# Modulation vectors of a two-block transformer: the product on VectorE, the sum over blocks on GpSimd

## The chip, the core and the metric

One core of one Trainium2 chip. The metric is the device time of one execution in microseconds (us), the median of three runs. Engines are called as the profile calls them: PE (TensorE's matmuls) and PEld (its weight loads), DVE (VectorE), ACT (ScalarE), POOL (GpSimd), SP (SyncE, which issues the DMAs). A matmul here has 128x128 weights and up to 512 columns.

## What is computed

A transformer block with sparse and latent attention, and behind it a second block whose norms and residuals are modulated by vectors that depend on a conditioning vector `c` (for the tokens) and `c_ctx` (for the context). The part that the change touches:

```
mod_lat = silu(c)     @ w_mod + b_mod        # w_mod: 1024 x 9216
mod_ctx = silu(c_ctx) @ w_mod + b_mod
ml, mc  = split(mod_lat, 9), split(mod_ctx, 9)
x  = x  + 0.5 * ml[2] * swiglu(modulate(rms_norm(x,  g), ml[0], ml[1]), w_in, w_out)
cx = cx + 0.5 * mc[2] * swiglu(modulate(rms_norm(cx, g), mc[0], mc[1]), w_in, w_out)
```

These two vector-matrix products depend on nothing that the first block computes, so the kernel does them while the first block runs: a feed-forward layer (ffn1), attention with its projections, `w_out`, and a second feed-forward layer (ffn2). All arithmetic is float32; the large matmuls are done as three passes on a high part and a low part of each operand.

## The kernel before

**Weights.** A weight tile of 128x2048 comes from memory into `RAW` (SP). ACT copies it rounded into `WH` (line 1080), DVE writes the rest `RAW - WH` into `WL` (line 1361, in `split`). Then PE runs on it. There are two buffers of each; while PE runs step b, ACT and DVE make the weights of step b + 1.

**Steps.** ffn1 and ffn2 have 34 steps each. `gate_up` is a step that makes one block of 128 hidden units (48 matmuls of 512 columns); after it ACT applies silu (line 1126, into `SA`), DVE multiplies (line 1437, into `VA`, which frees the PSUM banks), and POOL splits the result into `HH` (line 1845) and `HL` (line 1847). `down` (`pairs` on PE and SP) is a step that adds two blocks of the output to `X` (DVE, line 1460). The order is: 8 gate_up, 4 down, 8 gate_up, 4 down, 6 gate_up, 4 down; the last four have 36 matmuls, all others 48. Between ffn1 and ffn2 stand the attention and the four down steps of `w_out`.

**Norms.** During the last four down steps of a layer ACT squares the finished blocks of `X` (line 1095) and POOL adds six of these squares to the first (`norm`, line 1871). PE sums over partitions when the last addition is there (line 610); the next layer waits for that.

**Modulation vectors.** `w_mod` is cut into 72 tiles of 1024x128, held in `MW` as 128 partitions x 8 blocks x 128 columns. Each of the 34 steps of ffn1, the 4 of `w_out` and the 34 of ffn2 takes one tile. The first 46 tiles are multiplied by both vectors (`CV2[:, k, 0]` and `CV2[:, k, 1]`), the last 26 by one. The function `mods` exists on four engines:

- SP loads tile m + 2 into `MW` when tile m is done (semaphore `mod_s`);
- DVE, at the head of its step, multiplies block k by the scalar of each partition and adds it to the sum in `MACC` (a view of `RB`): one instruction of 128x128 for each block and vector, line 1417 for the first block and 1414 for the other seven. Each k waits for the one before;
- PE, behind the matmuls of its step, sums `MACC` over partitions (line 690, `pe.wait_ge(mod_s, ...)` at line 687), and then begins the next step;
- DVE copies the result into `MOD` at the end of its step (`mods_out`, line 1425), behind the semaphore `mod_done` of PE.

**Order.** Every engine runs its instructions in the order in which they are written, and `stage` makes rolled loops of most of them. So on DVE a step is: `mods`, `split`, the work on PE's result, `mods_out`. POOL has only `hidden` in a gate_up step, and nothing in a down step but the additions of `norm`, which stand behind a layer's last `hidden`.

Of the kernel before, what the change touches and what calls it, by code (L numbers as in the profile page):

```python
# [4 lines left out]
P = 128  # L5
# [54 lines left out]
def build(nc, inp, out):  # L60
    ctx = ExitStack()
    with ctx:
# [100 lines left out]
        mod_loaded = [sem(f"mod_loaded{s}") for s in range(2)]  # L163
        mod_s = sem("mod_s")
        mod_done, mod_out = sem("mod_done"), sem("mod_out")
# [68 lines left out]
        NCTX = 5 * KD  # L234
        MACC = RB[:, :].rearrange("p (t v c) -> p t v c", t=2, v=2)

        def vectors(m0):

            return 2 if m0 < NCTX else 1
# [209 lines left out]
        def _(sp):  # L449
# [8 lines left out]
            def mods(b0, j, s, m0):  # L458

                if m0 is None:  # L460
                    return
                if b0 == 0 and isinstance(j, int) and j < 2:
                    if j == 1:
                        for t in range(2):
                            sp.dma_start(MW[t][:, :, :], weights(inp["w_mod_2"][0], 0, KD, t * P, P))\
                                .then_inc(mod_loaded[t], 16)
                    return
                t = (s + b0) % 2
                if m0 == M0["wo"]:
                    sp.wait_ge(at_o, NG)  # L470
                if not (isinstance(j, int) and j + m0 < 2):
                    sp.wait_ge(mod_s, j * KD + KD * (m0 - 1))
                sp.dma_start(MW[t][:, :, :], weights(inp["w_mod_2"][0], 0, KD, j * P + m0 * P, P))\
                    .then_inc(mod_loaded[t], 16)
# [33 lines left out]
            for n in range(10):  # L508
                b = w_in_b + n
                s = b % 2  # L510
                sp.wait_ge(w_lo, b - 1)
                raw = RAW[s][:, :].rearrange("p (h k c) -> p h k c", h=2, k=KD)
                for half, (name, j, c) in enumerate(W_IN_TILES[2 * n:2 * n + 2]):
                    for c0, width, at in (MISC if name == "misc" else ((c, P, 0),)):
                        sp.dma_start(raw[:, half, :, at:at + width],
                                     w_in[:, c0:c0 + width].rearrange("(k p) n -> p k n", p=P)).then_inc(w_loaded[s], 16)
                if n == 0:
                    sp.wait_ge(pe_done, w_in_b)
                    sp.wait_ge(mod_s, KD * M0["wo"])
                    for dst, src in ((TA, "rope64"), (TB, "rope96"), (PERM, "perms")):  # L520
                        sp.dma_start(dst[:, :, :], inp[src]).then_inc(a_loaded, 16)
                    sp.dma_start(CM[:, :], inp["causal"]).then_inc(a_loaded, 16)
# [44 lines left out]
        def _(pe):  # L567
# [114 lines left out]
            def mods(b0, j, s, m0):  # L682
# [3 lines left out]
                t = (s + b0) % 2  # L686
                pe.wait_ge(mod_s, j * KD + KD * (m0 + 1))
                wait(pe, mod_out, after(j + m0, -1))
# [666 lines left out]
        def _(dve):  # L1355
# [46 lines left out]
            def mods(b0, j, s, m0):  # L1402
# [4 lines left out]
                dve.wait_ge(mod_loaded[t], j * 8 + (8 * (m0 - t) + 16))  # L1407
                for k in range(KD):
                    if k:
                        dve.wait_ge(mod_s, j * KD + (KD * m0 + k))  # L1410
                    for v in range(vectors(m0)):
                        o = MACC[:, t, v, :]
                        if k:
                            last = dve.scalar_tensor_tensor(out=o, in0=MW[t][:, k, :], scalar=CV2[:, k, v:v + 1],  # L1414
                                                            in1=o, op0=ALU.mult, op1=ALU.add)
                        else:
                            last = dve.tensor_scalar(o, MW[t][:, k, :], CV2[:, k, v:v + 1], None, ALU.mult)
                    last.then_inc(mod_s, 1)

# [418 lines left out]
        def _(pool):  # L1838
            def hidden(b0, n, tok, g0):

                for b, j, s, _ in stage(pool, b0, n):
                    pool.wait_ge(psum_free, b + 1)
                    h = HH[:, ds(j, 1), 0:tok].rearrange("p a t -> p (a t)")
# [4 lines left out]

            def ffn(stages, tok, g0):
                for kn, (bg, bd) in zip(CHUNKS, stages):  # L1850
                    hidden(bg, kn, tok, g0)
                    g0 += kn

            def branch(b0, h_to, l_to, y0):
# [9 lines left out]

            def norm(m):

                for k in range(1, m.n - 1):
                    pool.wait_ge(norm_sq, m.sq + k + 1)
# [15 lines left out]
            lows(norm1)  # L1884
            ffn(ffn1, T, 0)
            norm(norm_mix)
            lows(norm_mix)
            pool.wait_ge(ix_acc, 3 * IDX_HEADS)
            pool.memset(VB[:, :, :, :], 0.0).then_inc(v_zero, 1)
            norm(norm2)  # L1890
            lows(norm2)
            ffn(ffn2, T, H0["ffn2"])
            norm(norm_final)
            ffn(ffn3, T + TC, H0["ffn3"])
            norm(norm_x2)
            branch(bg_b, YH, YL, 0)
            branch(ba_b, MH, ML, KD)
            norm(norm_x3)
            ffn(ffn4, T, H0["ffn4"])
            norm(norm_out)  # L1900

# [72 lines left out]
```

## Time and profile before

| | |
|---|---|
| median of 3 runs | 2821.77 us (2820.44 to 2825.56) |
| the profiled execution | 2822.73 us, of which the span in the trace is 2820.9 us |
| PE busy | 2709.4 us (96%) |
| DVE, ACT, POOL busy | 1421.5, 757.6, 346.7 us |

The span is the time from the first to the last instruction in the trace; the 1.8 us around it are in the measured time too. "Busy" adds the durations of an engine's instructions. A timeline row gives the start in us from the span's start, the duration in us (of all instructions that it merges), engine, line, operation, what it writes and reads, and in brackets how long the engine had stood idle before and what ended that. An instruction's duration includes what it waits inside for memory ports.

### The profile page before, as it was taken

The page shows a single profiled execution, that of the slowest core. Times are in us where ns is not written, and L with a number is a line of the kernel's source. Part 1 is how long each engine was busy: PE and PEld are TensorE (multiplying, and loading weights), DVE is VectorE, ACT ScalarE, POOL GpSimd, SP SyncE. Part 2 cuts the span into 40 slices and gives each one's busy share as a digit, 9 for nine tenths or more (in the row PEclk, how much of TensorE's full clock was granted, in tenths as well). Part 3 has the DMA queues.
Part 4 walks back from the last instruction along what each step waited for, and adds up shares of the span by engine and source line. Part 5 has one row for each costly group of instructions (what it writes and reads, how often), then busy time and mean ns, then how long its engine had stood idle before and what let it go on. Part 6 is the DMA issues. An engine that isn't in the chain of part 4 may idle for free.

```text
span 2820.9 us, 34194 instructions
## 1 busy us (share of the span) xinstructions
PE 2709.4 (96%) x12500; PEld 2168.7 (77%) x12500; DVE 1421.5 (50%) x2491; ACT 757.6 (27%) x1029; POOL 346.7 (12%) x259
## 2 busy tenths in 40 slices
PE   8999989888899999998999999999999999999998
PEld 6888877644457888878888888878888756888887
DVE  7877784556647756673122222254324653433333
ACT  3111232235542112133111111222322352321213
POOL 2111120000002101111211301200200002210102
PEclk9999999869699999987999999999999999999999
DMA  6444432200034454431212221222332001323331
GB/s 181 135 134 144 135 116 74 54 15 1 0 102 115 135 142 147 130 109 37 67 60 60 60 75 56 64 75 90 90 105 83 31 1 60 90 90 98 96 97 67
DMA packets 394763, 241.12 MB, mean 85 GB/s; under 512 B 14768, under 2 KB 392752, under 8 KB 394672
## 3 DMA queue, kind: packets, MB, share of 16 engines
q1 hardware_dynamic: 394672, 239.92, 29.1%
q8 instruction: 55, 0.90, 0.1%
q14 instruction: 36, 0.29, 0.0%
HBM read 237.79 MB, written 2.10 MB: 85 GB/s over the span
## 4 chain that ended last, share of the span: by engine, by line
PE 88%; DVE 7%; ACT 4%; issue 1%; DMA 1%; POOL 0%; SPq 0%; DVEq 0%; ACTq 0%; POOLq 0%
PE PS L669 22%; PE PS L676 21%; PE PS L671 21%; PE PS L656 3%; PE PS L653 3%; PE PS L654 3%; PE PS L1053 2%; PE PS L810 1%; PE PS L610 1%; DVE RB L1414 1%; PE PS L1033 1%; PE PS L896 1%; DVE WL L1361 1%; PE PS L876 1%; PE PS L903 1%
## 5 line engine op out<-in xcount | busy, mean ns | idle before, releaser
L669 PE MATMUL PS<-NH,WH 128*128 128x512 f32 (+1 forms) x2128 | 626.0, 376 | 10.6 <-DVE WL L1361 6.3
L671 PE MATMUL PS<-NH,WL 128*128 128x512 f32 (+1 forms) x2128 | 620.1, 373 | 0.0
L676 PE MATMUL PS<-NL,WH 128*128 128x512 f32 (+1 forms) x2128 | 591.5, 372 | 0.0
L1361 DVE TENSOR_TENSOR WL<-RAW,WH 128x2048 fp32r<-128x2048 f32 x190 | 462.0, 2432 | 103.6 <-ACT WH L1080 103.1
L1080 ACT ACTIVATE WH<-RAW 128x2048 fp32r<-128x2048 f32 x190 | 363.7, 1914 | 540.0 <-PE PS L676 501.0
L669 PEld LDWEIGHTS PS<-NH,WH 128*128 128x128 f32 x2128 | 384.0, 189 | 79.3 <-issue 9.0
L671 PEld LDWEIGHTS PS<-NH,WL 128*128 128x128 f32 x2128 | 389.3, 189 | 72.2
L676 PEld LDWEIGHTS PS<-NL,WH 128*128 128x128 f32 x2128 | 389.5, 189 | 71.9
L1414 DVE SCALAR_TENSOR_TENSOR RB<-MW,CV,RB 128x128 f32<-128x128 f32 x826 | 329.2, 431 | 17.8
L1126 ACT ACTIVATE SA<-PS 128x512 f32<-128x512 f32 x104 | 62.0, 596 | 663.1 <-PE PS L676 630.6
L669 PE MATMUL PS<-HH,WH 128*128 128x512 f32 (+1 forms) x820 | 237.5, 371 | 1.9 <-DVE WL L1361 1.9
L671 PE MATMUL PS<-HH,WL 128*128 128x512 f32 (+1 forms) x820 | 235.1, 368 | 0.0
L1845 POOL CAST HH<-VA 128x512 f32 (+2 forms) x88 | 58.6, 666 | 1332.3 <-DVE VA L1437 1332.3
L676 PE MATMUL PS<-HL,WH 128*128 128x512 f32 (+1 forms) x820 | 222.1, 368 | 0.0
L1437 DVE TENSOR_TENSOR VA<-SA,PS 128x512 f32<-128x512 f32 x88 | 60.4, 686 | 245.5 <-ACT SA L1126 245.5
L1847 POOL TENSOR_TENSOR HL<-VA,HH 128x512 f32 (+2 forms) x88 | 168.5, 1914 | 14.2 <-POOL HH L1845 14.0
L676 PEld LDWEIGHTS PS<-HL,WH 128*128 128x128 f32 x820 | 148.8, 189 | 26.6
L671 PEld LDWEIGHTS PS<-HH,WL 128*128 128x128 f32 x820 | 148.5, 188 | 26.6
L669 PEld LDWEIGHTS PS<-HH,WH 128*128 128x128 f32 x820 | 146.1, 188 | 25.9 <-DVE WL L1361 2.1
L1436 DVE TENSOR_TENSOR VA<-SA,PS 128x256 f32<-128x256 f32 x22 | 9.3, 421 | 271.7 <-ACT SA L1126 271.7
L653 PE MATMUL PS<-NH,WH 128*128 128x512 f32 x320 | 127.3, 398 | 0.0
L654 PE MATMUL PS<-NL,WH 128*128 128x512 f32 x320 | 122.2, 384 | 0.0
(268 smaller groups left out, 2691.6 us busy)
## 6 DMA issues: line engine op xcount, KB each, us to landing
RAW<-in_ffn_w_in SPq DMA_DIRECT2D x88, 512.0 KB, 4.8
MW<-in_w_mod SPq DMA_DIRECT2D x72, 512.0 KB, 3.7
RAW<-in_w_in SPq DMA_DIRECT2D x70, 512.0 KB, 4.1
RAW<-in_w_gate SPq DMA_DIRECT2D x44, 512.0 KB, 4.2
RAW<-in_w_up SPq DMA_DIRECT2D x44, 512.0 KB, 5.4
RAW<-in_w_down SPq DMA_DIRECT2D x32, 512.0 KB, 4.3
RAW<-in_ffn_w_out SPq DMA_DIRECT2D x32, 512.0 KB, 4.3
RAW<-in_w_out SPq DMA_DIRECT2D x16, 512.0 KB, 4.4
```

The costliest lines, as they stand in the source:

```text
L653: pe.matmul(o, wh, xh(k), start=k == 0, stop=False)
L654: pe.matmul(o, wh, xl(k), start=False, stop=False)
L656: last = pe.matmul(o, wl, xh(k), start=False, stop=k == kn - 1)
L669: pe.matmul(outs[half][x], w[half][0], xh(k), start=k == 0, stop=False)
L671: pe.matmul(outs[half][x], w[half][1], xh(k), start=False, stop=False)
L676: last = pe.matmul(outs[half][x], w[half][0], xl(k), start=False, stop=k == kn - 1)
L1080: act.activation(WH[1 - s][:, :], RAW[1 - s][:, :], ACT.Copy).then_inc(w_hi, 1)
L1126: act.activation(SA[:, s, 0:T], G[s][:, :], func).then_inc(gate_done, 1)
L1361: dve.tensor_tensor(WL[1 - s][:, :], RAW[1 - s][:, :], WH[1 - s][:, :].bitcast(F32), ALU.subtract).then_inc(w_lo, 1)
L1414: last = dve.scalar_tensor_tensor(out=o, in0=MW[t][:, k, :], scalar=CV2[:, k, v:v + 1], in1=o, op0=ALU.mult, op1=ALU.add)
L1437: dve.tensor_tensor(VA[:, s, 0:T], SA[:, s, 0:T], U[s][:, :], ALU.mult).then_inc(psum_free, 1)
L1847: pool.tensor_tensor(l, VA[:, s, 0:tok], h.bitcast(F32), ALU.subtract).then_inc(h_split, 1)
```

## The change

On DVE `mods` becomes one multiplication of 128x1024 for each vector: the whole tile times `CV2` broadcast along the 128 columns. The product with the last (or only) vector is written in place into `MW`, that with the first of two into a part of `CX`, a buffer that is otherwise not in use until ffn2 is over (`product`). It signals `mod_p`.

POOL gets a `mods` of its own: it adds the eight blocks in three halvings (4 blocks onto 4, 2 onto 2, 1 and 1 into `MACC`), for both vectors in turn, waits between the halvings for its own results (`mod_t`), and signals `mod_s` at the end. It also waits for `mod_done` of the tile before last. `mods` stands ahead of `hidden` in a gate_up step, and is all that POOL does in a down step (`down`); in the last four down steps the additions of `norm` are now written between the tiles' sums: one behind the second tile, two behind the third, three behind the fourth. The counts in the waits on `mod_s` go down from eight for each tile to one. PE's instructions stay as they are.

```diff
 # semaphores, and the place of the product
+        mod_p, mod_t, mod_s = sem("mod_p"), sem("mod_t"), sem("mod_s")
+        def product(t, v, m0):
+            return MW[t][:, :, :] if v == vectors(m0) - 1 else CX[:, 4 * t:4 * t + 4, :].rearrange("p a (b c) -> p (a b) c", b=2)
...
 # SP, mods
-                    sp.wait_ge(mod_s, j * KD + KD * (m0 - 1))
+                    sp.wait_ge(mod_s, j + (m0 - 1))
...
 # PE, mods
-                pe.wait_ge(mod_s, j * KD + KD * (m0 + 1))
+                pe.wait_ge(mod_s, j + (m0 + 1))
...
 # DVE, mods
-                for k in range(KD):
-                    if k:
-                        dve.wait_ge(mod_s, j * KD + (KD * m0 + k))
-                    for v in range(vectors(m0)):
-                        o = MACC[:, t, v, :]
-                        if k:
-                            last = dve.scalar_tensor_tensor(out=o, in0=MW[t][:, k, :], scalar=CV2[:, k, v:v + 1],
-                                                            in1=o, op0=ALU.mult, op1=ALU.add)
-                        else:
-                            last = dve.tensor_scalar(o, MW[t][:, k, :], CV2[:, k, v:v + 1], None, ALU.mult)
-                    last.then_inc(mod_s, 1)
+                for v in range(vectors(m0)):
+                    last = dve.tensor_tensor(product(t, v, m0), MW[t][:, :, :],
+                                             CV2[:, :, v:v + 1].to_broadcast([P, KD, P]), ALU.mult)
+                last.then_inc(mod_p, 1)
...
 # POOL
+            def mods(b0, j, s, m0, t0):
+
+                if m0 is None:
+                    return
+                t, nv = (s + b0) % 2, vectors(m0)
+                pool.wait_ge(mod_p, j + (m0 + 1))
+                if not (isinstance(j, int) and j + m0 < 2):
+                    pool.wait_ge(mod_done, j + (m0 - 1))
+                for n, w in enumerate((4, 2)):
+                    for v in range(nv):
+                        p = product(t, v, m0)
+                        pool.tensor_tensor(p[:, 0:w, :], p[:, 0:w, :], p[:, w:2 * w, :], ALU.add).then_inc(mod_t, 1)
+                    pool.wait_ge(mod_t, j * (2 * nv) + (t0 + (n + 1) * nv))
+                for v in range(nv):
+                    p = product(t, v, m0)
+                    last = pool.tensor_tensor(MACC[:, t, v, :], p[:, 0, :], p[:, 1, :], ALU.add)
+                last.then_inc(mod_s, 1)
...
+            def down(b0, m0, t0, m=None):
+
+                for b, j, s, _ in stage(pool, b0, KD // 2, True):
+                    mods(b0, j, s, m0, t0)
+                    if m is not None and j:
+                        norm(m, 2 * j - 2, 2 * j)
...
                 for b, j, s, _ in stage(pool, b0, n):
+                    mods(b0, j, s, m0, t0)
                     pool.wait_ge(psum_free, b + 1)
```

In the rows below the line numbers of before and after differ by a few. DVE, around the second step of ffn1, before (`RB` is where `MACC` lies, `CV` is `CV2`):

```order
L1437 TENSOR_TENSOR VA<-SA,PS 128x512
L1425 COPY MOD<-PS 128x2
L1417 TENSOR_SCALAR RB<-MW,CV 128x128 x2
L1414 SCALAR_TENSOR_TENSOR RB<-MW,CV,RB 128x128 x14
L1361 TENSOR_TENSOR WL<-RAW,WH 128x2048
L1437 TENSOR_TENSOR VA<-SA,PS 128x512
L1425 COPY MOD<-PS 128x2
```

and now:

```order
L1434 TENSOR_TENSOR VA<-SA,PS 128x512
L1422 COPY MOD<-PS 128x2
L1413 TENSOR_TENSOR CX<-MW,CV 128x1024
L1413 TENSOR_TENSOR MW<-MW,CV 128x1024
L1365 TENSOR_TENSOR WL<-RAW,WH 128x2048
L1434 TENSOR_TENSOR VA<-SA,PS 128x512
L1422 COPY MOD<-PS 128x2
```

The sixteen small instructions between the copy into `MOD` and the making of `WL` have become two large ones, and nothing else on DVE has moved.

POOL, one gate_up step in the rolled loop of ffn1, with the semaphores that the instructions wait for, before:

```order
L1845 ISA [waits psum_free]
L1845 COPY HH<-VA 128x512
L1847 REGISTER_ALU [waits pool_s]
L1847 TENSOR_TENSOR HL<-VA,HH 128x512
L1842 REGISTER_ALU
```

and now:

```order
L1847 TENSOR_TENSOR CX<-CX 128x512 [waits mod_done]
L1847 TENSOR_TENSOR MW<-MW 128x512
L1848 ISA
L1847 TENSOR_TENSOR CX<-CX 128x256 [waits mod_t]
L1847 TENSOR_TENSOR MW<-MW 128x256
L1848 REGISTER_ALU
L1851 TENSOR_TENSOR RB<-CX 128x128 [waits mod_t]
L1851 TENSOR_TENSOR RB<-MW 128x128
L1872 ISA [waits psum_free]
L1872 COPY HH<-VA 128x512
L1874 REGISTER_ALU [waits pool_s]
L1874 TENSOR_TENSOR HL<-VA,HH 128x512
```

Six additions with three waits for other work or for POOL's own results stand ahead of the split of the hidden block.

POOL, the end of ffn1, before:

```order
L1847 TENSOR_TENSOR HL<-VA,HH 128x512
L256 REGISTER_ALU
L256 COMPARE_AND_BRANCH
L1871 TENSOR_TENSOR VA<-VA,SA 128x512 [waits norm_sq]
L1871 TENSOR_TENSOR VA<-VA,SA 128x512 [waits norm_acc,norm_sq] x5
L1878 TENSOR_TENSOR NL<-VA,NH 128x512 [waits norm_hi] x3
```

and now:

```order
L1906 TENSOR_TENSOR VA<-VA,SA 128x512 [waits norm_acc,norm_sq] x2
L1847 TENSOR_TENSOR CX<-CX 128x512 [waits mod_done,mod_p]
L1847 TENSOR_TENSOR MW<-MW 128x512
L1847 TENSOR_TENSOR CX<-CX 128x256 [waits mod_t]
L1847 TENSOR_TENSOR MW<-MW 128x256
L1851 TENSOR_TENSOR RB<-CX 128x128 [waits mod_t]
L1851 TENSOR_TENSOR RB<-MW 128x128
L1906 TENSOR_TENSOR VA<-VA,SA 128x512 [waits norm_acc,norm_sq] x3
L1913 TENSOR_TENSOR NL<-VA,NH 128x512 [waits norm_hi] x3
```

The additions of squares, which stood alone behind the last split, now stand behind the sums of tiles; the last three wait behind those of the last tile.

## Rows read from the trace of the kernel before

**Rows 1.** Page, part 1: busy time, share, instructions of each engine.

```profile
PE 2709.4 (96%) x12500; PEld 2168.7 (77%) x12500; DVE 1421.5 (50%) x2491; ACT 757.6 (27%) x1029; POOL 346.7 (12%) x259
```

**Rows 2.** Timeline, TensorE, one step of ffn1: start us, us, work [idle before].

```profile
66.55 0.50 PE L690 MATMUL PS<-ones,RB 128*128 128x1 f32 x4
...
77.90 0.50 PE L690 MATMUL PS<-ones,RB 128*128 128x1 f32 x4
```

**Rows 3.** Timeline, VectorE, the same step.

```profile
67.38 0.69 DVE L1437 TENSOR_TENSOR VA<-SA,PS 128x512 f32<-128x512 f32 x1 [1.82 <-ACT SA L1126]
68.05 0.89 DVE L1417 TENSOR_SCALAR RB<-MW,CV 128x128 f32<-128x128 f32 x2
68.97 5.55 DVE L1414 SCALAR_TENSOR_TENSOR RB<-MW,CV,RB 128x128 f32<-128x128 f32 x14
74.44 2.28 DVE L1361 TENSOR_TENSOR WL<-RAW,WH 128x2048 fp32r<-128x2048 f32 x1
```

**Rows 4.** Timeline, GpSimd, the same step.

```profile
68.24 0.61 POOL L1845 CAST HH<-VA 128x512 f32 x1 [8.94 <-DVE VA L1437]
69.02 1.45 POOL L1847 TENSOR_TENSOR HL<-VA,HH 128x512 f32 x1 [0.17 <-POOL HH L1845]
```

**Rows 5.** Group of line 1414: shortest, median, longest in ns.

```profile
L1414 DVE SCALAR_TENSOR_TENSOR RB<-MW,CV,RB x826: 337/351/1493, 26.1 to 1245.7; 128x128 f32<-128x128 f32 x166
```

**Rows 6.** Timeline, VectorE and GpSimd, ffn3 and then ffn4.

```profile
1334.12 2.45 DVE L1361 TENSOR_TENSOR WL<-RAW,WH 128x2048 fp32r<-128x2048 f32 x1 [0.70 <-ACT WH L1080]
...
1334.60 3.69 POOL L1847 TENSOR_TENSOR HL<-VA,HH 128x768 f32 x1 [0.17 <-POOL HH L1845]
...
2482.89 3.35 DVE L1361 TENSOR_TENSOR WL<-RAW,WH 128x2048 fp32r<-128x2048 f32 x1 [1.03 <-ACT WH L1080]
...
2482.80 1.29 POOL L1847 TENSOR_TENSOR HL<-VA,HH 128x512 f32 x1 [0.16 <-POOL HH L1845]
```

**Rows 7.** Timeline, one 128x1024 instruction of VectorE, one of GpSimd.

```profile
13.00 1.22 DVE L1501 TENSOR_TENSOR WL<-RAW,WH 128x1024 fp32r<-128x1024 f32 x1
...
14.38 2.36 POOL L1882 TENSOR_TENSOR WL<-RAW,WH 128x1024 fp32r<-128x1024 f32 x1 [13.93 <-ACT WH L1171]
```

**Rows 8.** Timeline, start of ffn1: VectorE, then TensorE.

```profile
25.56 0.48 DVE L1417 TENSOR_SCALAR RB<-MW,CV 128x128 f32<-128x128 f32 x2 [1.65 <-ACT CV L1176]
30.51 2.28 DVE L1361 TENSOR_TENSOR WL<-RAW,WH 128x2048 fp32r<-128x2048 f32 x1
...
31.09 0.50 PE L690 MATMUL PS<-ones,RB 128*128 128x1 f32 x4
32.85 0.72 PE L669 MATMUL PS<-NH,WH 128*128 128x512 f32 x2 [1.25 <-DVE WL L1361]
```

**Rows 9.** Timeline, TensorE, last down stage of ffn1 and what follows.

```profile
372.15 0.73 PE L669 MATMUL PS<-HH,WH 128*128 128x512 f32 x2 [1.28 <-DVE WL L1361]
...
392.12 0.50 PE L653 MATMUL PS<-HH,WH 128*128 128x512 f32 x1 [1.59 <-DVE WL L1361]
...
400.45 0.61 PE L690 MATMUL PS<-ones,RB 128*128 128x1 f32 x4
405.26 1.02 PE L610 MATMUL PS<-ones,VA 128*128 128x1 f32 x4 [4.20 <-POOL VA L1871]
```

**Rows 10.** Timeline, GpSimd, squares added in that stage.

```profile
394.01 2.73 POOL L1871 TENSOR_TENSOR VA<-VA,SA 128x512 f32<-128x512 f32 x2 [7.81 <-ACT SA L1095]
```

**Rows 11.** Timeline, TensorE, w_out: first step, and after the last.

```profile
830.16 0.73 PE L669 MATMUL PS<-NH,WH 128*128 128x512 f32 x2 [0.94 <-DVE WL L1361]
...
865.98 0.72 PE L610 MATMUL PS<-ones,VA 128*128 128x1 f32 x5 [1.57 <-POOL VA L1871]
```

**Rows 12.** Timeline, TensorE, start of ffn2.

```profile
885.75 0.84 PE L690 MATMUL PS<-ones,RB 128*128 128x1 f32 x4 [2.11 <-DVE RB L1414]
888.06 1.19 PE L669 MATMUL PS<-NH,WH 128*128 128x512 f32 x2 [1.47 <-DVE WL L1361]
```

**Rows 13.** Stretches: PE, PEld, DVE, ACT, POOL busy us, PEclk, DMA share, GB/s.

```profile
888.00:892.00 4.00, 3.94 (x9) 3.13 (x10) 3.89 (x10) 0.00 (x0) 2.05 (x2) 0.50 0.91 266
```

More of the change, by code:

```diff
@@ L163, in build @@
         mod_loaded = [sem(f"mod_loaded{s}") for s in range(2)]
-        mod_s = sem("mod_s")
+        mod_p, mod_t, mod_s = sem("mod_p"), sem("mod_t"), sem("mod_s")
         mod_done, mod_out = sem("mod_done"), sem("mod_out")
@@ L518, in _ @@
                     sp.wait_ge(pe_done, w_in_b)
-                    sp.wait_ge(mod_s, KD * M0["wo"])
+                    sp.wait_ge(mod_s, M0["wo"])
                     for dst, src in ((TA, "rope64"), (TB, "rope96"), (PERM, "perms")):
@@ L1838, in _, with adds, hidden @@
         def _(pool):
-            def hidden(b0, n, tok, g0):
+            def mods(b0, j, s, m0, t0):
[14 more added lines that the diff above has]
+                last.then_inc(mod_s, 1)
+            def adds(m0, n):
+                return 0 if m0 is None else 2 * vectors(m0) * n
+            def down(b0, m0, t0, m=None):
[3 more added lines that the diff above has]
+                        norm(m, 2 * j - 2, 2 * j)
+            def hidden(b0, n, tok, g0, m0=None, t0=0):
                 for b, j, s, _ in stage(pool, b0, n):
+                    mods(b0, j, s, m0, t0)
                     pool.wait_ge(psum_free, b + 1)
@@ L1847, in hidden, with ffn @@
                     pool.tensor_tensor(l, VA[:, s, 0:tok], h.bitcast(F32), ALU.subtract).then_inc(h_split, 1)
-            def ffn(stages, tok, g0):
-                for kn, (bg, bd) in zip(CHUNKS, stages):
-                    hidden(bg, kn, tok, g0)
+            def ffn(stages, tok, g0, m=None, m0=None, t0=0):
+                for c, (kn, (bg, bd)) in enumerate(zip(CHUNKS, stages)):
+                    hidden(bg, kn, tok, g0, m0, t0)
+                    t0 += adds(m0, kn)
+                    m0 = None if m0 is None else m0 + kn
+                    if m0 is not None or c == 2:
+                        down(bd, m0, t0, m if c == 2 else None)
+                    t0 += adds(m0, KD // 2)
+                    m0 = None if m0 is None else m0 + KD // 2
                     g0 += kn
+                norm(m, KD - 2, KD - 1)
+                return t0
             def branch(b0, h_to, l_to, y0):
@@ L1863, in branch, with norm @@
                             .then_inc(y_split, 1)
-            def norm(m):
-                for k in range(1, m.n - 1):
+            def norm(m, k0=1, k1=KD - 1):
+                for k in range(max(k0, 1), k1):
                     pool.wait_ge(norm_sq, m.sq + k + 1)
@@ L1884, in _ @@
             lows(norm1)
-            ffn(ffn1, T, 0)
-            norm(norm_mix)
+            t0 = ffn(ffn1, T, 0, norm_mix, M0["ffn1"])
             lows(norm_mix)
@@ L1889, in _ @@
             pool.memset(VB[:, :, :, :], 0.0).then_inc(v_zero, 1)
-            norm(norm2)
+            down(wo_b, M0["wo"], t0, norm2)
+            t0 += adds(M0["wo"], KD // 2)
+            norm(norm2, KD - 2, KD - 1)
             lows(norm2)
[L1892 to L1895, printed above, removed]
+            ffn(ffn2, T, H0["ffn2"], norm_final, M0["ffn2"], t0)
+            ffn(ffn3, T + TC, H0["ffn3"], norm_x2)
             branch(bg_b, YH, YL, 0)
@@ L1898, in _ @@
             norm(norm_x3)
-            ffn(ffn4, T, H0["ffn4"])
-            norm(norm_out)
+            ffn(ffn4, T, H0["ffn4"], norm_out)
 def _vectors(inputs):
```

## The prediction

> **What bounds the kernel now.** I read part 1 of the page first: PE is busy for 2709 of 2821 us, DVE for half, POOL for 12% [rows 1]. Then the timeline of one ordinary step, engine by engine, then the places where PE waits.
>
> In an ordinary step PE sets the pace. It comes to the modulation matmuls at 66.55 and again at 77.90, 11.35 us later [rows 2], and waits for nothing. DVE's work on modulation in this step begins at 68.05 and is 6.4 us long; `WL` follows at 74.44 and ends at 76.72 [rows 3]. `mod_s` is thus there at 74.5, 3.4 us before PE asks, and `WL` 1.2 us before. DVE is nearly full, but not late. What leaves it earns nothing here; what comes to lie between 66.5 and 77.9 in a chain may cost.
>
> DVE is late at a few places. At the start PE is ready after 31.6 and waits 1.25 for `WL` [rows 8]. In the last down stage of ffn1, whose steps have 36 matmuls instead of 48, it waits 1.28 and 1.59, and once between them about half as long [rows 9]. In `w_out` it is 0.94 [rows 11], at the start of ffn2 2.11 and 1.47 [rows 12]. With some 2 of the 4.20 at the end of ffn1 [rows 9], where DVE makes `WL` before it finishes `X`, all that an unloaded DVE could give is about 12 us.
>
> **What DVE and POOL cost each other.** Two pairs of rows show that an instruction of DVE with two SBUF inputs and one of POOL don't overlap [rows 6]. In ffn3 `HL` was issued at 1334.60 while `WL` ran to 1336.57; it took 3.69, to 1338.29, 1.72 from the end of `WL`. In ffn4 `HL` was first, and ended at 2484.09; `WL`, issued at 2482.89, took 3.35 instead of 2.28 and ended at 2486.24, 2.15 after it. Each holds the other for its whole length; who asked first goes first. `HL` in an ordinary step waits only for one small instruction (1.45 instead of 1.29) [rows 4, 6], since DVE's are 0.35 short; but the longest of those is 1.49, an addition of POOL longer [rows 5]. I take it that an instruction which reads PSUM and one SBUF operand has no part in this. The Trainium skill says the same as a rule ("SBUF — State Buffer", section "Who interferes with whom"): the pair of ports is locked for the whole instruction when DVE has two SBUF inputs and GpSimd reads SBUF. By that rule, the trace agrees, the product of the change is such an instruction, since `CV2` lies in SBUF too.
>
> **The prices.** DVE: a 128x1024 instruction with two SBUF inputs is 1.22 [rows 7], 1.14 apart when they follow one another: 2.3 for a tile with two vectors, where 6.4 (5.0 undisturbed, 25.56 to 30.6 [rows 8]) goes away. A broadcast operand is not in the trace; it could only make this longer. POOL: 128x512 took 1.29 [rows 6], 128x1024 2.36 [rows 7], so 0.2 + 2.1 ns for each column. I have no row of 256 or 128 columns; by this line they are 0.74 and 0.47. The sum of a tile for two vectors is then 2 x (1.29 + 0.74 + 0.47) = 5.0, with two waits of POOL for itself of 0.17 [rows 4] 5.3; I use 5.1, for one vector 2.8. Bounds: the second of two additions may begin inside the first, or all be 0.1 shorter; or each small one may have a floor nearer to 512's.
>
> **Ordinary gate_up steps with two vectors.** The chain from PE's last matmul E: DVE is free for the product at E + 1.5 (68.05 against 66.55). Products with POOL's cast of 0.6 between them: to E + 4.4. `HL`, which waited at the port: to E + 5.6. `WL`, issued behind the product: to E + 7.7. Only then the sums, to E + 12.8; PE has its next matmuls done at E + 11.35. So PE waits about 1.4, and the modulation matmul moves from before anything that waits to the end of the chain. In the step behind such a late one, DVE starts the product when its copy into `MOD` is done, 0.7 behind the modulation matmul M, and the chain gives M + 11.55 against M + 11.38: 0.2 more. Two steps cost 1.6, one 0.8. There are 22 such steps in ffn1 (the first apart) and 8 in ffn2: 21 x 0.8 = 17, 7 x 0.8 = 5.5.
>
> **Down steps** have no split of POOL: products, `WL`, sums give E + 1.5 + 2.3 + 2.2 + 5.1 = E + 11.1. They just fit: 0. **Steps with one vector** have 3.4 us less: 0.
>
> **The starts.** ffn1: products 25.56 to 27.9, `WL` to 30.1, sums to 35.2, then 0.5 of modulation matmuls: PE goes on at 35.8 instead of 32.85, +3.0 [rows 8]. That DVE makes `WL` 2.5 us sooner doesn't help, because PE's modulation matmuls stand ahead of step 2. `w_out`: the same, against 830.16: +2.0. ffn2, where DVE comes to the tile behind a norm, against 888.06: +3.0.
>
> **The last down stages.** ffn1, from modulation matmul to modulation matmul. POOL now adds squares behind each sum, and these (two of 1.37, [rows 10]) take port time from the next product: 0.7 + 2 squares and 2 products in turn to 4.6, `WL` to 6.8, sums to 11.9. With one pair, with one addition and with none that is 11.9, 10.9, 10.5, in all 33.3 where the trace has 30.1 (from 372.15 - 1.28 - 0.5 to 400.45 [rows 9]); into the stage another +3.4 (12.0, where 36 matmuls and their modulation matmuls need 8.6). Behind the last one come three squares, 4.1, where the trace waits 4.8 to 405.26 [rows 9]: -0.7. Together +6.0. `w_out`: +0.9 in the last step, and 4.1 instead of 2.1 from its last modulation matmul to 865.98 [rows 11], +1.9: +2.8. ffn2, one vector: +1.9.
>
> **SP** now loads tile m + 2, and behind it the weights of the next step, when POOL has done tile m, so near the end of a step instead of its middle. They are wanted almost a whole step later, so I count 0.
>
> **Sum.** 3.0 + 17 + 6.0 (ffn1) + 2.0 + 2.8 (`w_out`) + 3.0 + 5.5 + 1.9 (ffn2) = 41. Overlap of two additions by 0.1 takes 7 off, by the same chain; all additions 0.1 shorter would take 16. On the other side PE's restart: modulation matmuls behind a wait took 0.84, otherwise 0.50 [rows 2, 12], about 0.3 in a dozen steps, +4; and the clock was at half (0.50, 1.2 GHz) at 888 to 892 after PE had stood [rows 13], so the waits at the starts, now of 4 and 6 us, may cost as much again. I take **+38**. The profiled execution (2822.73, span 2820.9) lies 1 us above the median; the forecast goes on the median: 2821.8 + 38 = **2860**.
>
> **Rivals.**
> *It costs much more.* If an addition of 256 or 128 columns costs as much as 512 on POOL, 1.3, every sum is 2.7 longer, also the down steps are late (1.9 each) and the gate_up steps 3.0: the same chain gives +145. With 0.2 more for each, +65. Against: 2.36 for 1024 leaves a fixed part of only 0.2. 12% for over +55.
> *Faster.* If the small additions slip in between DVE's instructions and PE finds `mod_s` in time, what is left is DVE's lateness, up to 12 us of it; with the last stage and the starts half won, -8, 2814. It decides at the start: the sums must be done by 32.8, 4.9 us behind the product, with `WL` in the same time and ports. The Trainium skill speaks for this side ("VectorE: DVE Perf Modes", section "Rules for kernel authors"): chained DVE instructions should become few, and the sixteen do become two. For: DVE's time falls by 200 us. Against: [rows 6] leave 5.1 + 2.2 in a row. 8%.
> *It nearly fits.* With additions 0.3 shorter than I have them, the chain of a gate_up step ends inside PE's matmuls, and only starts and ends of layers cost: +3, and up to +5.6 it can't be told from nothing. 11%.
> *Forecast*, +6 to +55: 69%.
>
> **Numbers.** Within 0.2% (5.6 us, about what a measurement of this kernel can tell from no change): 0.11. Faster by more: 0.08. Slower by more: 0.81. The range is 2824 to 2890: it leaves out the faster case, a part of the near fit, and the upper half of the costly one.
>
> **What the profile would show.** PE's wait list gets an entry for line 690 behind POOL's last addition, some 20 to 30 us in all, with waits of 1 to 1.5 in every second gate_up step with two vectors and none where one vector is left. DVE busy falls by about 200 us, POOL's rises by 250 to 300. `WL` or the additions are stretched where they meet. The start of step 2 is at 35.8. POOL's additions read 1.3, 0.74 and 0.47. I am wrong if two-vector steps of 11.35 remain (the chain is shorter than I have it), if down steps are late too (small additions have a floor), or if PE waits for weights from memory.

## The result, and the profile of the changed kernel

The changed kernel takes **2867.8 us** (2859.1 to 2870.9, 4 runs), the kernel before beside it 2821.1 (2818.9 to 2825.6). The ratio is 1.0159, 95% interval 1.0132 to 1.0185: 1.3 to 1.9% slower. The execution profiled after the change took 2870.9 us with a span of 2868.8, so 47.9 us more than the span of before.

Page, part 1, of after (answers [rows 1]):

```profile
PE 2733.5 (95%) x12500; PEld 2180.8 (76%) x12500; DVE 1244.3 (43%) x1665; ACT 757.4 (26%) x1029; POOL 821.7 (29%) x613
```

DVE has 177 us less and POOL 475 more. Of POOL's, about 290 are additions as they last undisturbed (an estimate: 46 tiles at 2 x (1.28 + 0.74 + 0.46), 26 at half of that); most of the rest is time in which an instruction of POOL stood at the memory port behind one of DVE. The groups of the new instructions, on POOL and DVE, shortest, median and longest in ns:

```profile
L1847 POOL TENSOR_TENSOR CX<-CX x92: 722/1014/3341, 28.6 to 1012.4; 128x512 f32<-128x512 f32 x46, 128x256 f32<-128x256 f32 x46
L1851 POOL TENSOR_TENSOR RB<-CX x46: 452/460/464, 34.7 to 1013.9; 128x128 f32<-128x128 f32 x46
L1413 DVE TENSOR_TENSOR CX<-MW,CV x46: 1211/1216/2221, 26.2 to 1003.9; 128x1024 f32<-128x1024 f32 x46
```

256 columns are 0.72 to 0.74 on POOL, 128 are 0.46, and the product with its broadcast operand is 1.22, as any 128x1024 instruction [rows 7].

**One gate_up step.** Timeline of after, first PE, then DVE, then POOL, from the modulation matmuls of one step to those of the next (answers [rows 2 to 4]):

```profile
48.67 0.51 PE L694 MATMUL PS<-ones,RB 128*128 128x1 f32 x4
61.16 0.61 PE L694 MATMUL PS<-ones,RB 128*128 128x1 f32 x4 [0.98 <-POOL RB L1851]
72.92 0.61 PE L694 MATMUL PS<-ones,RB 128*128 128x1 f32 x4
...
50.18 1.22 DVE L1413 TENSOR_TENSOR CX<-MW,CV 128x1024 f32<-128x1024 f32 x1
51.31 1.64 DVE L1413 TENSOR_TENSOR MW<-MW,CV 128x1024 f32<-128x1024 f32 x1
52.87 3.38 DVE L1365 TENSOR_TENSOR WL<-RAW,WH 128x2048 fp32r<-128x2048 f32 x1
...
51.95 2.15 POOL L1874 TENSOR_TENSOR HL<-VA,HH 128x512 fp32r<-128x512 f32 x1
54.06 3.33 POOL L1847 TENSOR_TENSOR CX<-CX 128x512 f32<-128x512 f32 x1
57.36 1.29 POOL L1847 TENSOR_TENSOR MW<-MW 128x512 f32<-128x512 f32 x1
58.73 0.74 POOL L1847 TENSOR_TENSOR CX<-CX 128x256 f32<-128x256 f32 x1
...
60.65 0.46 POOL L1851 TENSOR_TENSOR RB<-MW 128x128 f32<-128x128 f32 x1
```

Read it as one row at a port. `HL` is issued while the second product runs (to 52.95) and ends 1.15 behind it, at 54.10. `WL`, issued at 52.87, ends 2.15 behind `HL`, at 56.25. The first addition, issued at 54.06, lasts 3.33, because it ends 1.14 behind `WL`. Then the other five follow, and PE, ready at 60.2, goes on at 61.16. The step has taken 12.49 us instead of 11.35; the one behind it takes 11.76 and shows no wait.

**Where the 47.9 us are.** Distances to the same instruction of before, at the modulation matmuls and the sums of the norms:

| stretch | forecast | measured |
|---|---|---|
| start of ffn1, to the second tile | 3.0 | 4.8 |
| two-vector gate_up steps of ffn1 | 17 | 16.4 |
| two-vector down steps of ffn1 | 0 | 0.0 |
| last down stage of ffn1, to the norm's sums | 6.0 | 6.7 |
| attention | 0 | -0.5 |
| `w_out`, start | 2.0 | 4.9 |
| `w_out`, rest, to the norm's sums | 2.8 | 2.2 |
| norm2 and start of ffn2 | 3.0 | 5.9 |
| two-vector steps of ffn2 | 5.5 | 5.2 |
| one-vector steps of ffn2 | 0 | 0.0 |
| last down stage of ffn2, to the norm's sums | 1.9 | 1.2 |
| all behind it | 0 | 0.9 |

The starts are larger than forecast. Timeline of PE in after, the first tile of ffn1, of `w_out`, and of ffn2 (answers [rows 8], [rows 11], [rows 12]), and of the stretches behind the three waits (busy us of PE, PEld, DVE, ACT, POOL, then PEclk; answers [rows 13]):

```profile
35.59 0.61 PE L694 MATMUL PS<-ones,RB 128*128 128x1 f32 x4 [3.74 <-POOL RB L1851]
...
858.96 1.01 PE L694 MATMUL PS<-ones,RB 128*128 128x1 f32 x4 [2.52 <-POOL RB L1851]
...
927.07 1.00 PE L694 MATMUL PS<-ones,RB 128*128 128x1 f32 x4 [6.05 <-POOL RB L1851]
```

```profile
35.50:40.00 4.50, 4.41 (x14) 3.56 (x15) 3.77 (x4) 0.00 (x0) 2.13 (x4) 0.62 0.76 217
859.00:866.00 7.00, 7.00 (x19) 5.70 (x20) 4.63 (x4) 1.67 (x3) 3.48 (x2) 0.51 0.74 218
927.00:935.00 8.00, 7.93 (x23) 6.41 (x24) 5.11 (x4) 0.00 (x0) 5.46 (x4) 0.56 0.74 197
```

In all three TensorE was granted half its clock (1.2 instead of 2.4 GHz) for most of the stretch, which makes the means of 0.51 to 0.62 above; before, the clock was full at the first two. At the start of ffn1 a part of the 4.8 is no effect of the change: the first product began at 26.17, where the first multiplication of before began at 25.56, because PE had waited 5.9 us for the input instead of 5.1.

### The profile page after: what moved, and what is told of

It is laid out like the page before. It is cut to its first block, busy times and chain, and to the rows that moved or that the text cites. A ratio compares the mean times of both kernels' runs of the same rounds, so it can differ in the third digit from the quotient of the medians.

```text
span 2868.8 us, 33435 instructions
## 1 busy us (share of the span) xinstructions
PE 2733.5 (95%) x12500; PEld 2180.8 (76%) x12500; DVE 1244.3 (43%) x1665; ACT 757.4 (26%) x1029; POOL 821.7 (29%) x613
## 4 chain that ended last, share of the span: by engine, by line
PE 75%; issue 9%; POOL 6%; DVE 6%; ACT 3%; DMA 1%; DVEq 0%; POOLq 0%; SPq 0%; ACTq 0%
PE PS L673 19%; PE PS L680 19%; PE PS L675 19%; POOL CX L1847 3%; PE PS L657 2%; PE PS L660 2%; PE PS L658 2%; POOL MW L1847 2%; PE PS L1057 2%; PE PS L614 1%; PE PS L1037 1%; DVE MW L1413 1%; PE PS L880 1%; PE PS L900 1%; DVE VA L1399 1%
## 5 line engine op out<-in xcount | busy, mean ns | idle before, releaser
L1365 DVE TENSOR_TENSOR WL<-RAW,WH 128x2048 fp32r<-128x2048 f32 x190 | 486.1, 2559 | 106.1 <-ACT WH L1084 105.6
L1872 POOL CAST HH<-VA 128x512 f32 (+2 forms) x88 | 85.9, 977 | 843.2 <-DVE VA L1434 843.2
L1847 POOL TENSOR_TENSOR CX<-CX 128x512 f32<-128x512 f32 x92 | 182.4, 1982 | 294.0 <-DVE MW L1413 290.4
L1874 POOL TENSOR_TENSOR HL<-VA,HH 128x512 f32 (+2 forms) x88 | 214.1, 2433 | 14.4 <-POOL HH L1872 14.2
L1847 POOL TENSOR_TENSOR MW<-MW 128x512 f32<-128x512 f32 (+1 forms) x144 | 171.5, 1191 | 58.6 <-DVE MW L1413 56.6
```

The source lines that it names most:

```text
L1365: dve.tensor_tensor(WL[1 - s][:, :], RAW[1 - s][:, :], WH[1 - s][:, :].bitcast(F32), ALU.subtract).then_inc(w_lo, 1)
L1847: pool.tensor_tensor(p[:, 0:w, :], p[:, 0:w, :], p[:, w:2 * w, :], ALU.add).then_inc(mod_t, 1)
L1872: pool.tensor_copy(h, VA[:, s, 0:tok]).then_inc(pool_s, 1)
L1874: pool.tensor_tensor(l, VA[:, s, 0:tok], h.bitcast(F32), ALU.subtract).then_inc(h_split, 1)
```

## The experiments

All times are medians of four to eleven runs; the kernel before ran beside each (2820.9, 2820.2 and 2820.8 in the three groups). The last column of the table is read from the profiles: how much later than in the kernel before PE ends the matmuls of ffn2's last step. What lies behind that is the same code in all. It took 1565 to 1575 us in the profiles of this case, so a difference between two spans is no finer than some us, and this column is finer.

| kernel | us | ratio to before (95%) | at ffn2's end |
|---|---|---|---|
| changed | 2867.8 | 1.0132 to 1.0185 | +46.6 |
| one_vector | 2816.6 | 0.9976 to 1.0002 | -7.1 |
| halving_out | 2820.0 | 0.9992 to 1.0020 | +2.2 |
| halving_twice | 2921.3 | 1.0339 to 1.0374 | +100.2 |
| sums_on_dve | 2820.3 | 0.9986 to 1.0005 | +0.7 |
| pe_later | 2819.9 | 0.9985 to 1.0012 | +3.0 |
| first_on_dve | 2828.5 | 1.0014 to 1.0045 | +9.1 |
| filled_waits | 2856.8 | 1.0102 to 1.0144 | +37.1 |
| first_on_dve_later | 2818.0 | 0.9973 to 0.9999 | -3.2 |
| later_wl_first | 2850.7 | 1.0094 to 1.0122 | +29.0 |
| half_later_wl_first | 2824.9 | 0.9999 to 1.0018 | +7.5 |
| dve_later_wl_first | 2823.1 | 0.9994 to 1.0018 | +0.2 |
| before_later_wl_first | 2818.9 | 0.9985 to 1.0004 | +0.9 |

**The length of the chain.** The theory (A): PE asks for a sum that ends a row of instructions at the port, and that row is 1.4 us too long. The rival (B): the loss goes with the time that POOL's work adds.

```diff
 # one_vector, for DVE and POOL
-            return 2 if m0 < NCTX else 1
+            return 1
 # halving_out
-                for n, w in enumerate((4, 2)):
+                for n, w in enumerate((4,)):
 # halving_twice
-                for n, w in enumerate((4, 2)):
+                for n, w in enumerate((4, 2, 2)):
```

> The changed kernel, but only one vector is multiplied and added for every tile; PE keeps both of its modulation matmuls and sums the same row twice (the vectors for the context are left out of what is computed). Theory A: PE waits because product, WL and sums run in a row at the memory port (E + 12.8 us against a step of 11.35, E being PE's last matmul of the step before). Here the row is 1.14 + 2.5 us shorter, E + 9.1, so the waits of all gate_up steps go (21.6 us as measured: 16.4 in ffn1, 5.2 in ffn2), most of the 4.5 at the start and of the 6.7 at the end of ffn1, and some 8 around w_out and the start of ffn2: 2826 us (2815 to 2835), PE's waits for POOL's sums under 5 us in all. Theory B: what costs is that POOL's and DVE's instructions are stretched by each other, in proportion to the time that POOL adds. Half of the additions are left: 2868 - 46/2 = 2845 us.

> The changed kernel without its second halving (256 columns); blocks 2, 3, 6 and 7 are left out of the sums. Theory A (a chain that is 1.4 us too long): two additions of 0.74 are 1.5 us, and the chain ends at E + 11.3, just inside the step. The 21.6 us of the gate_up steps go, and 1.5 us at each of about six late places (three starts, the last down steps of ffn1, w_out): 2868 - 21.6 - 9 = 2837 us (2830 to 2843). Theory B (in proportion to POOL's added time, of which 30% goes): 2868 - 14 = 2854 us.

> The changed kernel with its second halving done twice (the sums hold two of the partial sums twice, so the vectors are others). Theory A: the chain is 1.5 us longer, now late in every gate_up step with two vectors: from modulation matmul to modulation matmul 11.55 + 1.5 = 13.05 us, where the two lengths of now have a mean of 12.1. 28 steps give 27 us; 8 down steps, until now just in time, 0.45 each, 4 us; the last down stage of ffn1 4.5, w_out 3, three starts 4.5; steps with one vector nothing. 2868 + 43 = 2911 us (2900 to 2920). Theory B: + 14, 2882 us.

A holds and B falls: 1.5 us off a sum of 5 gave back 48 us, 1.5 us more cost 53. The waits of PE that end with a sum, in the kernel without the second halving and in that with two:

```profile
PE PS L694 <- POOL RB L1851: 10.9, 5, 4.6
```

```profile
PE PS L694 <- POOL RB L1851: 68.8, 35, 8.0
```

(us in total, times, longest; in the changed kernel 31.3, 25 and 6.0.) Without the halving the 28 gate_up steps cost 1.1 us instead of 21.6. With two, I had every late step at 13.05 and came out 10 too low, and the clock is the likely reason. Two steps behind a wait of 1.92 ran at full clock (1.00 from 207 to 232.9), in 12.80 and 13.25, as expected. But in much of ffn1 and in ffn2 steps of 14.0 and 13.1 alternate, with waits of 2.5 to 2.6 in every second one, and behind most of these the clock was half for some 3 to 4 us. One of them, PE, POOL's last addition for the next tile, and the stretch behind the wait:

```profile
260.29 0.61 PE L694 MATMUL PS<-ones,RB 128*128 128x1 f32 x4 [2.60 <-POOL RB L1851]
273.45 0.50 PE L694 MATMUL PS<-ones,RB 128*128 128x1 f32 x4
...
272.55 0.46 POOL L1851 TENSOR_TENSOR RB<-MW 128x128 f32<-128x128 f32 x1
...
260.30:266.00 5.70, 5.70 (x20) 4.60 (x21) 4.71 (x4) 0.00 (x0) 3.16 (x3) 0.70 0.72 218
```

The step takes 13.16 though its sum is done at 273.01, before PE has done its matmuls: PE at half clock sets it, not the chain. Such a pair is 27.1, the one at full clock 26.05; ten waits in gate_up steps (1.6 to 2.6 us) had the half clock behind them, and at about 1 us each they are the 10 us (an estimate from these two pairs; no run fills these waits). The other misses have one sign too: what the shorter chain saved outside the gate_up steps was 24 us, not 9, above all 14 between the end of ffn1 and the start of ffn2. More on this below.

**The products or the sums.**

```diff
 # sums_on_dve: behind the products, on DVE; POOL has no mods
+                dve.wait_ge(mod_p, j + (m0 + 1))
+                for n, w in enumerate((4, 2)):
+                    for v in range(nv):
+                        p = product(t, v, m0)
+                        dve.tensor_tensor(p[:, 0:w, :], p[:, 0:w, :], p[:, w:2 * w, :], ALU.add).then_inc(mod_t, 1)
...
```

> The products as in the changed kernel, but all three halvings on DVE, and POOL has no modulation work; the additions of the norms stay where the changed kernel has them on POOL. It tells the large products (and their broadcast operand, and the new place of the norms' additions) from the move of the sums to POOL. Theory A: DVE's modulation work for two vectors is 2.3 + 2 x (0.65 + 0.37 + 0.22) + 0.2 of waits = 5.0 us, about what the sixteen small ones take undisturbed and 1.4 less than they take beside HL, and ends before WL: no wait of PE for sums. 2820 us (2812 to 2828). Rival: the products themselves, longer at the port than 0.35 us each, are what delays HL, WL and PE: then it stays over 2840 us.

As expected: the large products and the broadcast operand cost nothing, nor do the norms' additions in their new place as long as no sums stand in front of them; the move of the sums does. But DVE wins no time by them either. Its timeline, one two-vector tile in this kernel:

```profile
68.55 1.22 DVE L1413 TENSOR_TENSOR CX<-MW,CV 128x1024 f32<-128x1024 f32 x1
69.69 1.63 DVE L1413 TENSOR_TENSOR MW<-MW,CV 128x1024 f32<-128x1024 f32 x1
71.36 1.66 DVE L1422 TENSOR_TENSOR CX<-CX 128x512 f32<-128x512 f32 x1
...
74.86 2.28 DVE L1365 TENSOR_TENSOR WL<-RAW,WH 128x2048 fp32r<-128x2048 f32 x1
```

6.3 us from the first product to `WL`, where the sixteen small instructions took 6.4 [rows 3]: 0.5 and 1.0 of it is waiting behind POOL's cast and `HL`, which come between long instructions as between short ones.

**The place where PE asks.**

```diff
 # pe_later: PE (and DVE's copy into MOD alike)
             def mods(b0, j, s, m0):
-                t = (s + b0) % 2
...
+                if not (isinstance(j, int) and j + m0 in STARTS):
+                    sums(b0 - 1, j, s, m0 - 1)
+                if isinstance(j, int) and j + m0 in ENDS:
+                    sums(b0, j, s, m0)
```

> The changed kernel; PE's two modulation matmuls of tile m, and DVE's copy of their result, stand one step later, behind the matmuls of step m + 1 (the last tile of ffn1, of w_out and of ffn2 stays behind its own step). All work is the same, only the place at which PE asks for the sums. Theory A (PE loses time because it asks at the end of a chain that is 1.4 us too long): the 21.6 us of the gate_up steps go, 4.5 at the start, and some 5 at the starts of w_out and ffn2; the last down stages keep their loss, since the last tile is asked for at once. 2868 - 31 = 2837 us (2828 to 2845), two-vector steps of 11.35 to 11.45. Rival: product, WL, HL and sums together fill the memory port for 11.4 us of a step of 11.35, so that the steps stay above 11.7 wherever PE asks: over 2848 us.

The 21.6 us are gone, and so is the rival. Three of PE's modulation matmuls, and one first addition on POOL:

```profile
201.16 0.50 PE L704 MATMUL PS<-ones,RB 128*128 128x1 f32 x4
212.51 0.51 PE L704 MATMUL PS<-ones,RB 128*128 128x1 f32 x4
223.87 0.50 PE L704 MATMUL PS<-ones,RB 128*128 128x1 f32 x4
...
206.64 3.33 POOL L1863 TENSOR_TENSOR CX<-CX 128x512 f32<-128x512 f32 x1
```

The same work at the same port (the first addition of most tiles still lasts 3.2 to 3.3, of the others 1.3) fits into steps of 11.35. The forecast of 2837 was too high; the start gave 6.4 instead of 4.5, and from the end of ffn1 to the start of ffn2 12 came back instead of 5.

**The clock.** Three long waits stand in front of stretches at half clock. Filled with matmuls that nobody reads:

```diff
 # filled_waits: FILL = {0: 16, NF + 12: 10, M0["ffn2"]: 24}
+                if isinstance(j, int) and j + m0 in FILL:
+                    busy(FILL[j + m0])
                 pe.wait_ge(mod_s, j + (m0 + 1))
```

> The changed kernel; where PE waits 3.7, 2.5 and 6.1 us for the first tile of ffn1, of w_out and of ffn2, it first does 16, 10 and 24 matmuls of 128 columns that nobody reads. In the changed kernel the granted clock was 0.5 (1.2 GHz) for 3.4, 7 and 6 us after these waits. If the clock falls because PE stood idle, the matmuls behind run at full clock, and half of that time comes back, less what the filling overruns: 5 to 8 us less, 2861 us. Rival (the clock falls at such places anyway, as it also did at 888 us before): no difference, 2867 to 2870 us.

11 us less, and the granted clock behind all three places was full: at these places the clock falls because PE stands, and the rival falls. The stretches of this kernel that answer to those of after:

```profile
35.50:40.00 4.50, 4.50 (x23) 3.77 (x23) 4.06 (x4) 0.00 (x0) 2.12 (x3) 1.00 0.84 230
856.50:863.00 6.50, 6.50 (x30) 5.38 (x30) 4.63 (x4) 0.72 (x2) 3.88 (x2) 1.00 0.79 238
921.00:929.00 8.00, 8.00 (x38) 6.69 (x38) 5.62 (x4) 0.00 (x0) 5.46 (x4) 1.00 0.74 197
```

From these tiles' modulation matmuls to the next ones it is 11.47, 11.47 and 11.46, where the changed kernel has 13.08, 14.68 and 14.75. By place, in the profiles, the gain is 1.9 at the start (0.3 of it ahead of the first tile), 5.5 between the end of ffn1 and the second tile of ffn2, and 2.1 in the last down stage of ffn1, where nothing was filled: behind a wait of 2.94 the changed kernel had its half clock there too (0.53 at 395 to 402), this one, behind a wait of 2.88, did not. So a wait of that length can go either way, as in halving_twice above.

**Sharing the sums.** The first halving on DVE (in the second kernel with PE's matmuls one step later, and the norm's additions ahead of the sums):

```diff
 # first_on_dve, behind the products on DVE; POOL: enumerate((2,))
+                for v in range(vectors(m0)):
+                    p = product(t, v, m0)
+                    last = dve.tensor_tensor(p[:, 0:4, :], p[:, 0:4, :], p[:, 4:8, :], ALU.add)
+                last.then_inc(mod_p, 1)
 # first_on_dve_later, also: POOL, down
+                    if m is not None and j:
+                        norm(m, 2 * j - 2, 2 * j)
                     mods(b0, j, s, m0, t0)
```

> The changed kernel with the first halving (512 columns) on DVE right behind the products, and the second and third on POOL. The row of a two-vector tile is two additions of 1.29 shorter on POOL and two of 0.65 and a wait of 0.1 longer on DVE, 1.2 us less in all. By Theory A as it stands after the kernel without the second halving (1.5 us less: 2820) it is nearly enough: a wait of 0.2 is left in some gate_up steps, 3 us, and the late places cost 2 more: 2825 us (2820 to 2832). Rival: the long additions on DVE push HL and WL back by what they take off the sums, and it stays near the changed kernel, over 2845 us.

> The first halving on DVE and PE's modulation matmuls one step later together, and in the last down stages POOL's additions for the norm ahead of the tile's sums. Theory A: PE waits for no sum but at three ends of layers; the port is filled 10.2 us of 11.35, so WL and HL are in time. What is left against the kernel of before is the gain of an earlier WL at the start, at w_out and in the last down steps (4 us, as with one vector): 2816 us (2810 to 2822), a little faster than before. Rival (the port or DVE's longer row delay WL or HL): 2825 us or more.

Both as expected by A. With the halving shared, two-vector steps alternate between 11.5 and 11.35. With PE's question a step later as well no sum is late but at the ends of layers, the steps of 36 matmuls run in 8.63 (before: 8.64, 10.06, 9.52, 10.50), and the kernel's median is 2.2 us under that of before (ratio of the runs 0.9986, interval 0.9973 to 0.9999). It is the only one whose interval lies under 1, by a hair, and one of twelve such intervals may do so by chance: a gain is not shown. What the norm's additions ahead of the sums add isn't told apart either, since no run has them alone.

**The order on DVE.** In four kernels `split` stands ahead of `mods` and PE's matmuls one step later: with all sums on POOL, with the shared halving, with all on DVE, and with the instructions of the kernel before. The first three also have the norm's additions ahead of the sums.

```diff
 # DVE, gate_up and down
-                    mods(b0, j, s, m0)
                     split(s, b)
+                    mods(b0, j, s, m0)
```

> The changed kernel with PE's modulation matmuls one step later, DVE making WL ahead of the products, and POOL's additions for the norm ahead of the tile's sums in the last down stages. With the matmuls one step later alone: 2819.9. What the order adds: no product ahead of WL where DVE is late (in front of the first step of w_out and of ffn2, 1 to 2 us each), and squares that don't wait for 5 us of sums. 2816 us (2811 to 2821). Rival: HL and the products now come behind 2.3 us of WL, the port is as full as before, and nothing is won: 2820 us.

> The same with the first halving on DVE. Without WL first it was 2818.0. The gain of WL first as above, 2 us: 2816 us (2810 to 2820). If it is POOL's load that holds the ends of ffn1 and w_out, it is 2 us under the kernel with all sums on POOL; if DVE's lateness does, 2 us over it.

> Products and all sums on DVE (2820.3 in the old order), with PE's modulation matmuls one step later and WL first. PE's waits of before, 1.25 at the start, 1.3 + 1.6 + 0.7 in the last down stage of ffn1, 0.9 in w_out, 2.1 + 1.5 at ffn2, were waits for WL behind 5 to 6.4 us of modulation work. With WL first they go: 2820 - 8 = 2812 us (2808 to 2817). Rival (the gain comes from unloading DVE): over the kernels with sums on POOL.

> The kernel of before, sixteen small instructions for a tile and all, with only the two changes of order: PE's modulation matmuls one step later, WL first on DVE. If the order is what gains, and neither the products nor POOL's sums, it is as fast as the three kernels above: 2821 - 8 = 2813 us (2808 to 2818). Rival: the changed kernel's lighter DVE is worth 3 us or more beside it.

None gains what I expected, and the first is 31 us slower than pe_later, which has the product first (and the norm's additions behind the sums; first_on_dve_later has them ahead and loses nothing). Its timeline, ACT and then DVE in one step, and SP's issue of the tile and the weights:

```profile
210.52 1.92 ACT L1094 ACTIVATE WH<-RAW 128x2048 fp32r<-128x2048 f32 x1 [7.05 <-DMA RAW<-in_w_up]
...
212.47 2.29 DVE L1375 TENSOR_TENSOR WL<-RAW,WH 128x2048 fp32r<-128x2048 f32 x1 [8.12 <-ACT WH L1094]
...
203.09 0.37 SPq L480 DMA_DIRECT2D MW<-in_w_mod  x1
203.73 0.37 SPq L488 DMA_DIRECT2D RAW<-in_w_gate  x1
204.20 1.01 SPq L490 DMA_DIRECT2D RAW<-in_w_up  x1
```

DVE waits 8 us for `WH`, ACT 7 us for weights from memory. SP loads a tile when POOL's sum is done (`mod_s`), and the weights stand behind it in its queue. With `WL` first the sum ends later, the weights are late by as much, `WL` is late, and the products behind it make the next sum late. This is read from the timeline; no run gives the tiles another queue to test it. In PE's waits it shows as 25.7 us for sums, in 7 waits, most of it at the ends of ffn1 and `w_out`. ACT's waits for weights of gate, up and down in this kernel and in pe_later (us in total, times, longest):

```profile
ACT WH L1094 <- DMA RAW<-in_w_up: 137.8, 25, 15.5
ACT WH L1094 <- DMA RAW<-in_w_down: 101.6, 16, 12.9
```

```profile
ACT WH L1094 <- DMA RAW<-in_w_up: 18.7, 9, 5.9
ACT WH L1094 <- DMA RAW<-in_w_down: 11.7, 1, 11.7
```

In the changed kernel neither is there. The two kernels with all modulation work on DVE do win PE's waits for `WL`: they end the matmuls of the last step of ffn1 5.5 and 6.1 us earlier than before. They give it back to the last tile, whose sum is wanted at once: PE waits 6.5 and 6.1 us for it. That the lighter DVE gives nothing beside the order isn't shown by them, since with one_vector, where both engines have half the work, 7 us came by the last column (4 in the medians, with an interval that still holds 1).

## Why the prediction held, and where it was off

**The chain.** It was put at products E + 4.4, `HL` + 5.6, `WL` + 7.7, sums + 12.8; the step above has 4.3, 5.4, 7.6 and 12.4 (E = 48.67). The late step was put at 11.55 behind the modulation matmul and took 11.76. The pair is 24.25 against 24.35, 0.77 us for a step where 0.8 was said; that it is so close is partly luck, since the early step was put 0.3 too long and the late one 0.2 too short. Down steps fit, one-vector steps fit, both as said. In the first stage of ffn1 the waits are spread more evenly (steps of 12.0 to 12.3 behind the first pair), at the same sum.

**The rule on the port.** [rows 6] showed one engine held for the whole instruction of the other, and the 3.38 of `WL` and 3.33 of the addition are that again. The Trainium skill ("SBUF — State Buffer", section "Who interferes with whom") states it, and the trace agrees. With both engines always asking, the order in the step shown is alternate, each taking the port when the other's instruction ends, which is why DVE's `WL` didn't have to wait for all six additions, nor they slip in front of it.

**The rule on few instructions.** The rival "faster" rested on fewer instructions on DVE. The Trainium skill asks for that ("VectorE: DVE Perf Modes", section "Rules for kernel authors"). The runs show next to no gain from it: undisturbed, two products and six additions are 2.3 + 2.5 us against 5.0 for the sixteen, since a multiplication and an addition are now two instructions over the same columns; and sums_on_dve is as fast as before. The point from which that rival decided was the start: sums by 32.8. They ended at 35.53, 35.2 forecast.

**POOL's prices.** 1.29, 0.74 and 0.47 from a line through two rows; 1.28, 0.74 and 0.46 measured. The costly rival (a floor under small additions) and the near fit both needed other prices. The sums are 4.85 long behind `WL` where 5.1 was taken. For that, an overlap by 0.1, the forecast took 7 us off; but the late steps came out 0.2 longer than forecast and gave it back. The 7 off is the one term of the sum that found nothing to stand on: the pair is that of the 41.

**The starts: the term that was too small.** At the start of ffn1 PE went on at 36.06 where 35.8 was said, but what followed, mostly at half clock, cost 1.6 more. For PE's restart and the clock 4 us were written, and the clock itself was left to words ("may cost as much again"). filled_waits prices it at about 7.4 at the three places, and 9.5 with the fourth. By the table the three starts are 7.6 over their terms, and all else together is 1.1 under. That the forecast came out at 38 and not at 41 is the 7 taken off in vain, less those 4.

**Signs named beforehand.** PE's entry for the sum behind POOL's: 20 to 30 us said, 31.3 found, with waits of 0.8 to 1.1 in every second gate_up step (1 to 1.5 said), and in the first stage and in ffn2 shorter ones in almost every step. POOL +250 to 300 was said, +475 found: the record of an instruction counts its time at the port, which the forecast of this sign forgot though it had said it of [rows 4]. DVE -200 said, -177 found, for the same reason.

**SP.** Counted at 0, with "wanted almost a whole step later" as the cover. It held in the changed kernel. pe_later and above all later_wl_first show what that cover hides: a queue in which weights stand behind a wait for the sum.

**Still open.** Why some ends of layers gain so much from a shorter chain (14 us from the end of ffn1 to ffn2) is clear only in part. In halving_out 2.7 of it lie behind the first tile of `w_out`, where no wait and no half clock is left, and 1.0 behind that of ffn2, where PE still waits 4.62 and the clock is still half. Attention alone took between 401.5 and 408.0 us in the profiles, without a change in it, which blurs the rest.

## What to carry to other kernels

When work goes from one engine to another, write the chain from the last result to the consumer, with every instruction of both engines that shares the port in it, and compare its end with the moment when the consumer asks: 1.4 us too long, with what it did at the starts and ends of layers, was 47 us here, and 1.5 off it or one step of patience in PE's queue brought all of them back. Busy time tells nothing of that: DVE fell from 50% to 43%, POOL was at 29%. Price a wait of TensorE of 2 us or more with the half clock that may follow it, and look what is queued behind each semaphore that now comes later.

## What the runs showed of the hardware

- An operand broadcast along 128 columns (`CV2`, one value for each block) cost DVE nothing: 1.22 us for 128x1024.
- POOL's float32 addition goes with 0.2 us + 2.1 ns for each column, from 128 (0.46) over 256 (0.74) and 512 (1.28) to 1024 (2.36), without a floor.
- At the port the two engines take turns when both always have an instruction waiting: product, cast, product, `HL`, `WL`, addition.
- After waits of PE of 2.5 to 6.1 us at the starts of the changed kernel's layers the granted clock was half for most of the next 4.5 to 8 us; with 10 to 24 small matmuls in the wait it stayed full.
- Between 1.6 and 2.9 us it went either way. In halving_twice it was half behind waits of 1.63 and 2.60 (at 233 and 260) and full behind 1.92 and 2.42 (at 207 and 119); in filled_waits it was full behind 2.88 (at 393). After waits of about 1 us, which came in every second step, the matmuls went on at full clock.
